# Expert stage with six weight slots, all low parts on VectorE, and the first sorted block loaded ahead of weights

## What is computed

```python
    y = jax.nn.sigmoid(gate_dn) * y_dn + jax.nn.sigmoid(gate_sgu) * y_sgu
    return jnp.einsum("bld,de->ble", y, w_out)
...
    group_p, group_idx = lax.top_k(jax.nn.softmax(group_logits, axis=-1), 1)
...
    in_group = expert_logits[jnp.arange(n_tok), group_idx]
    exp_p, exp_idx = lax.top_k(jax.nn.softmax(in_group, axis=-1), TOP_K_IN_GROUP)
...
    h = jax.nn.silu(jnp.einsum("td,edf->tef", t, expert_w_gate)) \
        * jnp.einsum("td,edf->tef", t, expert_w_up)
    h = h * combine[:, :, None].astype(h.dtype)
    y = jnp.einsum("tef,efd->td", h, expert_w_down)
...
        h = layer_norm(DEEPNORM_ALPHA * h + mix, ln1_g[l], ln1_b[l])
...
        h = layer_norm(DEEPNORM_ALPHA * h + ffn, ln2_g[l], ln2_b[l])
```

## Time and profile before

| | |
|---|---|
| median of 3 runs | 2995.59 us (2990.28 to 2996.71) |
| profiled execution | 2997.38 us, span 2995.5 us |
| granted TensorE clock, mean | 0.941 |
| busy over the span | PE 89%, DVE 40%, ACT 23%, POOL 53% |
| expert stage, first product to last | 2650.3 to 2976.7 us |
| low parts of experts (page, section 5) | DVE 54 of 3365 ns mean, POOL 30 of 4635 ns mean |
| high parts of experts (page, section 5) | ACT 84 of 1913 ns mean |
| DMA over the span | 334.96 MB |

### The profile page before, as it was taken

How to read it: one execution, slowest core, us unless ns; L and a number is a source line. 1 busy time by engine, 2 the same in 40 slices (tenths; PEclk the granted TensorE clock), 3 DMA queues, 4 the chain that set the end, 5 groups by cost and what they waited for, 6 DMA issues and landing times. The chain is left out here.

```text
span 2995.5 us, 35985 instructions
## 1 busy us (share of the span) xinstructions
PE 2662.7 (89%) x14316; PEld 2238.9 (75%) x14316; DVE 1201.3 (40%) x1657; ACT 700.2 (23%) x1130; POOL 1573.3 (53%) x479
## 2 busy tenths in 40 slices
PE   5999999978999979997999979989899998658785
PEld 3888888866898848775888857879878977646564
DVE  4112011235774632076111243544231446448884
ACT  3111000113212411002100014334310111146563
POOL 2443555442642137764777755644367765145655
PEclk7999999988998999998999989989999999779998
DMA  5443221123220022231222233200032225167773
GB/s 232 201 178 135 67 70 66 49 96 137 70 71 32 1 100 88 96 113 56 94 92 102 79 115 121 93 9 1 1 135 104 94 90 199 51 254 302 266 292 122
DMA packets 52301, 334.96 MB, mean 112 GB/s; under 512 B 6500, under 2 KB 7524, under 8 KB 19344
## 3 DMA queue, kind: packets, MB, share of 16 engines
q1 hardware_dynamic: 50592, 327.44, 29.9%
q0 software_dynamic: 1584, 5.78, 0.5%
HBM read 314.84 MB, written 22.07 MB: 112 GB/s over the span
## 5 line engine op out<-in xcount | busy, mean ns | idle before, releaser
L160 POOL TENSOR_TENSOR whi<-raw,one_col 128x2048 fp32r<-128x2048 f32 (+2 forms) x160 | 533.7, 3336 | 952.7 <-PE bank L180 716.1
L163 POOL TENSOR_TENSOR wlo<-raw,whi 128x2048 fp32r<-128x2048 f32 (+2 forms) x160 | 707.9, 4425 | 12.6
L178 PE MATMUL bank<-uh_a,whi 128*128 128x512 f32 (+1 forms) x704 | 239.0, 339 | 14.8 <-DVE ul_a L600 14.8
L179 PE MATMUL bank<-ul_a,whi 128*128 128x512 f32 (+1 forms) x704 | 237.5, 337 | 0.0
L180 PE MATMUL bank<-uh_a,wlo 128*128 128x512 f32 (+1 forms) x704 | 237.1, 337 | 0.0
L3032 POOL TENSOR_TENSOR moe_wl<-moe_raw,moe_wh 128x2048 fp32r<-128x2048 f32 x30 | 138.8, 4635 | 136.8 <-ACT moe_wh L3139 136.6
L3200 DVE TENSOR_TENSOR moe_wl<-moe_raw,moe_wh 128x2048 fp32r<-128x2048 f32 x54 | 181.6, 3365 | 27.0 <-ACT moe_wh L3139 26.9
L3139 ACT ACTIVATE moe_wh<-moe_raw 128x2048 fp32r<-128x2048 f32 x84 | 160.5, 1913 | 59.1 <-PE bank L3088 30.8
L178 PEld LDWEIGHTS bank<-uh_a,whi 128*128 128x128 f32 x704 | 134.0, 190 | 34.4 <-issue 17.0
L178 PE MATMUL bank<-uh_b,whi 128*128 128x512 f32 x352 | 137.9, 392 | 7.6 <-DVE ul_b L600 6.6
L180 PEld LDWEIGHTS bank<-uh_a,wlo 128*128 128x128 f32 x704 | 134.0, 190 | 14.2
(11 more groups left out here) (552 smaller groups left out, 6539.6 us busy)
## 6 DMA issues: line engine op xcount, KB each, us to landing
moe_raw<-moe_w_dram SPq DMA_DIRECT2D x84, 1024.0 KB, 6.1
cond_ring<-w_ada_dram SPq DMA_DIRECT2D x27, 1024.0 KB, 7.0
raw<-gu_a_dram SPq DMA_DIRECT2D x22, 1024.0 KB, 5.1
raw<-gu_b_dram SPq DMA_DIRECT2D x22, 1024.0 KB, 4.9
raw<-wqkv_dram SPq DMA_DIRECT2D x12, 1024.0 KB, 4.8
raw<-dn_a_dram SPq DMA_DIRECT2D x16, 704.0 KB, 4.1
raw<-dn_b_dram SPq DMA_DIRECT2D x16, 704.0 KB, 4.0
ada_w<-w_ada_dram SPq DMA_DIRECT2D x9, 1024.0 KB, 20.1
```

Source lines behind the costliest of these rows:

```text
L160: e.nc.gpsimd.tensor_tensor(e.whi[p][:, 0:f], e.raw[p][:, 0:f], e.one_col[:, 0:1].to_broadcast([P, f]), ALU.mult).then_inc(e.w_hi, 1)
L163: e.nc.gpsimd.tensor_tensor(e.wlo[p][:, 0:f], e.raw[p][:, 0:f], e.whi[p][:, 0:f].bitcast(F32), ALU.subtract).then_inc(e.w_split, 1)
L178: e.nc.tensor.matmul(out, wh, xh, start=first, stop=False)
L179: e.nc.tensor.matmul(out, wh, xl, start=False, stop=False)
```

## The change

- RING_W becomes 6. The six pairs of high and low buffers lie in the old product buffers, the place of y2h, the place of X and the place of `tok`; so ScalarE's `hi(4)` waits for the rows (`late.row_ready`) and `hi(5)` for the scatters. Y, sil, h, hh and hl move to other addresses.
- All low parts are on VectorE. GpSimd only issues the scatters.
- The last norm's gain and offset are folded into two `scalar_tensor_tensor` on VectorE in `centre`.
- SP loads XB(0) ahead of weight slot 6 and XB(1) ahead of slot 8. The norm's rows LNP are loaded at slot 12 and not 10.
- ScalarE and VectorE are written in another order, two steps ahead in A and B and one in D.
- The first four of the residual's eight pieces are turned and scaled ahead of the last slot of `w_sgu`, whose loop is written out straight.

```diff
-RING_RAW, RING_W = 6, 4
+RING_RAW, RING_W = 6, 6
...
     def act_body(act, i, p, g):
+        if act_last is not None and i == last_slot:
+            act_last(act)
         act.wait_ge(v_ready, 1 + i)
...
+    def pe_body(pe, p, i, ready):
+        if pe_last is not None and i == last_slot:
+            pe_last(pe)
+        return pe_feature_major(e, p, KT, 2, xh, xl, False, ready=ready)
...
+    def pe_first(self, pe):
+        for n in range(4):
+            self.pe_residual(pe, n)
+
+    def act_first(self, act):
+        for n in range(4):
+            self.act_residual(act, n)
...
-        pe.wait_ge(self.res_in, 16)
-        for n in range(2 * NCH):
-            residual(n)
+        for n in range(4, 2 * NCH):
+            self.pe_residual(pe, n)
...
-    w_at = [BASE + r * 8192 for r in range(6)] + [MAIN, MAIN + 8192]
+    w_at = [BASE, BASE + 16384, BASE + 32768, MAIN, MAIN + 114944, MAIN + 81920]
...
-    by_pool = [s in (2, 3) or key[0] == "D" for s, key in enumerate(order)]
...
-                if s == RING_RAW + RING_W:
+                if s == RING_RAW:
                     sp.wait_ge(scattered, 16 * NCH)
-                    for r in range(2):
-                        sp.dma_start(XB[r][:, :], e.dram["xs"][r * P:(r + 1) * P, :]).then_inc(xb_in[r], 16)
+                    sp.dma_start(XB[0][:, :], e.dram["xs"][0:P, :]).then_inc(xb_in[0], 16)
+                if s == RING_RAW + 2:
+                    sp.dma_start(XB[1][:, :], e.dram["xs"][P:2 * P, :]).then_inc(xb_in[1], 16)
...
-                if b == 0:
-                    pool.wait_ge(lnp_in, 16)
-                pool.wait_ge(norm_done, b + 1)
-                nc.gpsimd.tensor_tensor(Y[r][:, :], Y[r][:, :], LNP[:, 0:D], ALU.mult).then_inc(gain_done, 1)
-                pool.wait_ge(gain_done, b + 1)
-                nc.gpsimd.tensor_tensor(Y[r][:, :], Y[r][:, :], LNP[:, D:2 * D], ALU.add).then_inc(y_done, 1)
                 pool.wait_ge(y_done, b + 1)
...
-            for s in range(RING_W):
+            for s in range(4):
                 hi(s)
                 if s == 1:
                     route.act_second(act)
+            act.wait_ge(late.row_ready, NCH)
+            hi(4)
             x_hi(0)
+            act.wait_ge(scattered, 16 * NCH)
+            hi(5)
             for x in range(NSTEP + 1):
                 if x:
-                    silu(x - 1)
-                if x + 1 < NSTEP and slot["A", x + 1] >= RING_W:
-                    hi(slot["A", x + 1])
-                if x:
                     hidden(x - 1)
-                if x + 1 < NSTEP:
-                    if slot["B", x + 1] >= RING_W:
-                        hi(slot["B", x + 1])
-                if x < NSTEP and slot["D", x] >= RING_W:
-                    hi(slot["D", x])
+                if 0 < x < NSTEP - 2:
+                    hi(slot["A", x + 2])
+                if x < NSTEP:
+                    silu(x)
+                if x + 2 < NSTEP:
+                    hi(slot["B", x + 2])
                 if x % EPG == 1 and x > EPG:
                     root(x // EPG - 1)
                 if x % EPG == EPG - 1 and x // EPG + 1 < NBLK:
                     x_hi(x // EPG + 1)
+                if x + 1 < NSTEP:
+                    hi(slot["D", x + 1])
...
-                nc.vector.tensor_scalar(Y[r][:, :], Y[r][:, :], mv[r][:, 0:1], rs[r][:, :], ALU.subtract, ALU.mult
-                                        ).then_inc(norm_done, 1)
...
+                nc.vector.scalar_tensor_tensor(Y[r][:, :], Y[r][:, :], mv[r][:, 0:1], LNP[:, 0:D], ALU.subtract, ALU.mult
+                                               ).then_inc(gain_done, 1)
+                dve.wait_ge(gain_done, b + 1)
+                nc.vector.scalar_tensor_tensor(Y[r][:, :], Y[r][:, :], rs[r][:, :], LNP[:, D:2 * D], ALU.mult, ALU.add
+                                               ).then_inc(y_done, 1)
+
+            for n in range(4):
+                lo(n)
             x_lo(0)
+            for n in range(4, RING_W):
+                lo(n)
             for x in range(NSTEP + 1):
                 if x:
-                    gate(x - 1)
-                if x + 1 < NSTEP and slot["A", x + 1] >= RING_W:
-                    lo(slot["A", x + 1])
-                if x:
                     hidden_lo(x - 1)
-                if x + 1 < NSTEP and slot["B", x + 1] >= RING_W:
-                    lo(slot["B", x + 1])
+                if 0 < x < NSTEP - 2:
+                    lo(slot["A", x + 2])
+                if x < NSTEP:
+                    gate(x)
+                if x % EPG == 0 and x:
+                    evacuate(x // EPG - 1)
+                if x + 2 < NSTEP:
+                    lo(slot["B", x + 2])
                 if x % EPG == EPG - 1 and x // EPG + 1 < NBLK:
                     x_lo(x // EPG + 1)
+                if x + 1 < NSTEP:
+                    lo(slot["D", x + 1])
                 if x % EPG == 0 and x:
-                    evacuate(x // EPG - 1)
                     normalise(x // EPG - 1)
```

89 lines of the change are left out of this document (41 added, 48 removed).

## The result

| | median us | runs | profiled execution (span) |
|---|---|---|---|
| before | 2996.15 (2990.28 to 3003.17) | 4 | 2997.4 (2995.5) |
| after | 2964.44 (2961.77 to 2969.26) | 4 | 2964.7 (2962.9) |

What follows compares the result with a forecast made beforehand. GpSimd's lock on VectorE, not work, was taken to stall TensorE in the expert stage. Terms 0.7 - 15.6 - 7.5 - 7.9 - 4.5 - 3.3 = -38.1 us on 2997.4 gave 2959.3, range 2952 to 2966 us.

Steps and rivals of the forecast that it cites:

- The lock and VectorE's price: Expert stage: GpSimd's work lengthens VectorE's low parts; without it each takes 2.28 us, VectorE 37.9 us a block.
- Rival (e): Expert stage: low parts cost 3.37 us beside heavy DMA and TensorE traffic, not through GpSimd; slower, 3011 us; chance 0.05.
- The walk through a block: One expert block: TensorE stalls 3.2, 2.2 and 2.1 us behind VectorE's x_lo and hidden_lo; period 44.0 us with clock loss.
- The clock's 1.7: Each expert block: 1.7 us lost to TensorE's low clock level, chosen between bounds of 0 and 4.5.
- Six slots carry this ... with four slots the same order would stall: Expert stage: six weight slots put ScalarE 5 to 8 us further ahead, covering VectorE's bursts of 10 us.
- parts 1 and 2: Expert stage: low parts and norm moved to VectorE; pieces change by +0.7, -15.6 and -7.5 us.
- The last piece: Turn of block 6 to the last product: 64.0 to 56.5 us, with 2.3 for the clock.
- The first piece: First product to the turn of block 1: 26.8 to 27.5 us, as D(0) waits some 3 us.
- The first block: Start of the expert stage: loading the first sorted block ahead of weights brings the first product 7.9 us earlier.
- Rival (d): Expert stage's start: scatters at 2.75 us each beside busy VectorE lose the gain; 2964 to 2967 us; chance 0.06.
- The residual's half: Ahead of w_sgu's last slot: moving the residual's first half ends w_out2's first slot 4.5 us earlier, and this is kept.
- The tail: Last product to the end: norm operations on VectorE take 2.5 instead of 5.8 us; 18.8 becomes 15.5.

Runs made afterwards that it cites:

- e1: The kernel after with the residual's first half put back behind w_sgu's last slot: 2965.69 us, ratio 0.9899 to the kernel before.
- e4: The kernel before with all low parts and the norm's rows on VectorE, four slots, old order, first block still loaded late: 2972.07 us.
- e9: The kernel before with all low parts and the norm's rows on VectorE and the first block loaded ahead of weights; four slots, old order: 2959.18 us.
- e15: The kernel after with five slots, the next block's turn one expert step earlier and the last norm placed later on VectorE: 2975.67 us.
- e3: The kernel before with only the load order changed, XB(0) ahead of weight slot 6 and XB(1) ahead of slot 8: 2976.94 us.
- e13: e1 with 16 extra, later overwritten transposes ahead of w_sgu's last slot and w_sgu's loop written out straight: 2968.56 us.
- e14: The kernel after with only the last norm's two row passes back on GpSimd: 2968.62 us, ratio 0.9907 to the kernel before.
- e8: The kernel after with the next block's turn one expert step earlier and the last norm placed later on VectorE: 2924.18 us.
- e10: e9 with the turn of the next block one expert step earlier: 2944.88 us, ratio 0.9836 to the kernel before.

## Why the prediction was right, and where not

**The lock and VectorE's price: right.** 2286 ns for all 84 low parts against 2.28 in the sum; VectorE's load is 36.4 to 36.7 a block against 37.9. Rival (e), a price of 3.37 from the company of DMA and TensorE, is out: there was more traffic beside it than before (301 to 324 GB/s a period against 272 to 283 in the long ones), and TensorE was as busy.

**The walk through a block: right.** Three stalls of 3.13, 1.93 and 1.84 at the named places, each ending 0.1 us after the operation of VectorE that was named for it, and a period of 43.85 for 44.0. Most of this is due to listing VectorE's operations in order with their durations; the busy shares alone (VectorE 83%, TensorE 84%) would not have told. The clock's 1.7 came out too: TensorE's busy time is 36.9 here and 35.1 in a block at 1.00. That is in part luck. It was chosen between bounds of 0 and 4.5 by likeness to one block, whose stalls were 1.7, 0.6 and 2.0 in the window of the earlier trace rows and not 2.2, 0.6 and 2.0; and periods of e1, e4 and e9, with much the same stalls, had anything from 1.00 (35.3 us) to 0.89 (40.0 us).

**"Six slots carry this ... with four slots the same order would stall": wrong** as I used it. e9 with four slots and the old order equals the kernel after, and its stalls are at the gate, not for weights. The claim about this very order was right in its way, as e15 shows (50 us), but the order itself brought nothing here: the credit that parts 1 and 2 gave to the slots belongs to GpSimd's leaving. It did not harm the number, since both orders stall as much; that is luck. (By the kernel a high part waits for the product six or four slots back, and not five or three as recorded; the difference of two slots is the same.)

**The last piece: 58.3 for 56.5.** The clock was 0.94 in it. An estimate from the windows: 213 matmul records at the 35.1 us for 161 of a block at 1.00 make 46.4, so of its 50.3 us of TensorE time 3.9 went to the clock, where the term had 2.3. Why the clock was lower there is open. The first piece, 26.44 for 27.5, errs by 1 the other way.

**The first block: right,** 7.6 for 7.9. Rival (d) was there in part: e3, with the same load order but two low parts fewer on VectorE there, has scatters of 0.95 and 18.83 us from first low part to first product; the kernel after has 1.90 and 20.22, e9 20.30. VectorE's company costs 1.4 us; the forecast had 0.7.

**The residual's half: the step that failed** is "All later slots were fully busy on TensorE, so it is kept". Slot 0 ended 3.2 earlier (4.5 forecast) and 2.2 came back in the slots behind, through the granted clock, in every kernel that has this part and, but for e13 with transposes of its own there, in none that lacks it. A fully busy engine is not one at a constant clock, and a gain ahead of it need not pass through. Of the 4.5, two terms were short: the input's low part was complete at 2524.5, 1.3 us later than before (0.8 in the sum), as the v and y2l of the slot ahead took 10.1 us beside GpSimd's split of the weights and 8.8 before; and the rest of the slot took 10.2 us for 9.4, with a granted clock of 0.50 from 2525 to 2530. This and the short 4.5 are 3.5 of the 5.5 us by which the span's change missed; the last piece is another 1.8.

**The tail: right,** 15.59 for 15.5. In e14's trace it is the only thing that the norm's move to VectorE is worth.

## What to carry to other kernels

When stalls recur with the same length in every round on engines that have slack, write the steps of the busy engine in order and ask which operation stands ahead of the one that is waited for; moving two steps gave more here (40 us) than taking GpSimd's work away had (24), though a third of it came through the clock and was not in the reckoning. When a gain comes out as forecast, still compare the waits that were to go with those that went. Where two engines lock each other out, count the lock by what is queued without a pause on one of them: here a pause of 1 us decided 5 us a block. A ring's depth is worth what the order asks of it, so try depth and order together.

## What the runs showed of the hardware

- **A lock with two outcomes.** GpSimd and VectorE low parts (tensor_tensor, both inputs in SBUF) exclude each other; one VectorE low part took 3.85 or 9.78 by whether GpSimd paused, and a block 43.65 or 48.65. The Trainium skill ("SBUF — State Buffer", Who interferes with whom) states the lock for a GpSimd instruction that reads SBUF; the trace agrees.
- **Scatters beside low parts.** Issuing one took GpSimd 0.95 with VectorE idle, and beside its tensor_tensor 1.90 (start), 2.75 (blocks of the kernel before) or 3.08 (of the kernel after). Who starts first seems to count: in the kernel after the scatter of a block began 0.02 us behind a low part of VectorE and took 3.08, in e9 it began 0.03 us ahead of one and took 0.95. The same page speaks of descriptors held up by VectorE's two-port modes only, and says that tensor_tensor has none; the measurement goes further than the page.
- **The granted clock of a fully busy TensorE.** With no gap in its work the same slot ran at 1.00 in 15.06 us or at 0.90 in 16.54. A block's TensorE time came in steps, 35.1, 36.9, 38.6 and 40.0 us at 1.00, 0.96, 0.92 and 0.89: 1.4 to 1.8 us for each. In e8, with the least idle time, every period had 1.00; but e9 has blocks of 0.96 and of 1.00 with the same stalls, and e10 had 0.96 in all five with 3.8 us idle of 40.6, where the first whole block of the kernel before had 1.00 with 4.3 of 39.8. Of the two levels, 1.2 and 2.4 GHz, the means of a window show only the mixture. What decides was not found.
- **The load stream.** 367 GB/s over a block in e8, with the DMA engines at 0.93, and no high part waited for it.
